# Attention and HGRN2 values: four weight lots at once, 512 moving columns instead of 256, in a decoder trunk on one core

## Chip, core and metric

One core of one Trainium2 chip runs the whole program as one launch. The metric is device time in microseconds (us), lower is better.

## What is computed

Two layers of a hybrid decoder trunk, 512 tokens of width 1024, all in float32. Each layer is a half-step SwiGLU (1024 to 2816 and back), a mixing stage with four branches of width 512, and a second half-step SwiGLU:

```python
h = rms_norm(x, mix_norm[l])
p = h @ w_in[l]
p_m2, p_s5, p_dsa, p_hg = jnp.split(p, IN_SPLITS, axis=-1)
y_a, y_b = mamba2_branch(p_m2, ...), s5_branch(p_s5, ...)
y_c, y_d = dsa_branch(p_dsa, ...), hgrn2_branch(p_hg, ...)
proj = jnp.einsum("blgc,gcd->blgd", ys, w_branch[l])
gates = jax.nn.sigmoid(h @ w_gate[l]).reshape(b, L, N_BRANCHES, D_MODEL)
x = x + jnp.einsum("blgd,blgd->bld", gates, proj) @ w_out[l]
```

The change touches two of the projections in `h @ w_in`: the attention values `v` (512 columns) of `dsa_branch`, and the HGRN2 values `i` (512 columns, called `hv` here) of `hgrn2_branch`. Both are needed with the tokens on the partitions, so for them the activations are the stationary operand and the weights move.

## The kernel before

Every weight matrix is streamed as *lots* of 128 x 1024 values (512 KB) through a ring of four slots: SP issues the DMA into `raw`, ACT rounds the lot to `w_hi` (`split_hi`, L461), POOL or DVE forms `w_lo = raw - w_hi` (`split_lo`, L469), and TensorE (PE) then makes three passes, hi·hi, lo·hi and hi·lo. A normal lot of a projection is 8 K tiles x 3 passes = 24 matmuls of 512 token columns (`passes`, L615 to L617). Output number t goes to PSUM bank t % 4. PE waits until that bank is free (semaphores `free0` to `free3`) and counts `out_done` when a sum is complete; ACT or DVE empties the bank. Banks 4 to 7 serve the branches' own small matmuls. The weights of lot n+4 may be split only when PE has used lot n.

The order of the work of a mixing stage is a hand-written list of steps, `script()`. Each engine walks it in order and does its share of each step, so a step's place sets its place on all queues. The steps that matter here:

- `("pair", "v", i)`, `("pair", "hv", i)`: the token-by-token product (`gemm_tokens`, L643 to L645) for two lots, i and i+1. For each of four blocks of 128 tokens, the stationary operand is `h_hi[:, k, tok]` or `h_lo`, the moving one 2 x 128 weight columns. That is 96 matmuls of 256 columns, two per projection and so eight in all. Two blocks share a bank; both lots are released only at the pair's end. ACT copies the two banks out (L1806) and then splits two lots.
- `glu` i: two sums of 12 matmuls each (a linear one, then its gate) for the S5 branch. ACT takes the gate's bank with a tanh (`glu_th`, L1928). DVE frees the linear bank in `glu_mul` (`glu_y`, L2729). ACT and DVE make `y_hi` (L1797) and `y_lo` (L2554) in `glu_end`.
- `da_index` b: 8 small matmuls (L1012), ACT's `da_r` (L1963), and on DVE the scores `da_mb` (L2765 to L2772). `da_rope`, `da_norm`, `da_topk` are further steps of the attention branch, the first and last on DVE alone.
- `gate` and `branch`: projections by `w_gate` and `w_branch`; `branch` 1, 0 is the first user of the S5 result and waits for `y_done` before each of its first four K tiles.
- `lot` hf, hq, hg: HGRN2's forget, query and output-gate projections; `hg_gates` and `hg_head` are its recurrence, head by head.

Of the kernel before, what the change touches and what calls it, by code (L numbers as in the profile page):

```python
# [51 lines left out]
def script():  # L52
# [36 lines left out]
    s += [("s5_end",), ("lot", "qi", 1), ("da_rope", 0, 2, 4), ("lot", "k", 3), ("da_index", 1), ("da_square", 1), ("glu", 0)]  # L89
# [77 lines left out]
for _i, (_kind, _j) in enumerate(MIX):  # L167
    if _kind in ("v", "hv") and _j % 2 == 0:

        USED_AT[MIX0 + _i] += 1  # L170
        assert all((MIX0 + _i + _l * NLOT) % 4 != 3 for _l in range(DEPTH)), (_kind, _j, (MIX0 + _i) % 4)
# [45 lines left out]
def trunk(nc, x_in, positions, w_lots, par_in, s5_in, con_in, gamma_in, out, s5_taps, s5_ud, s5_wd):  # L217
# [5 lines left out]
    with ctx:  # L223
# [228 lines left out]

        def split_hi(act, n0, it=0, taken=False):
# [4 lines left out]
            if n0 >= 4 and not taken:  # L458
                act.wait_ge(S["out_done"], USED_AT[n0 - 4] + 4 * it + OUT.layer * OUT0[NLOT])
# [11 lines left out]
        LOADED = 16  # L471
# [119 lines left out]
        def _(pe):  # L591
# [38 lines left out]
            def gemm_tokens(n0, cols, lots=1):  # L630

                s, w = slot(n0), P * lots
                pe.wait_ge(S["lo_done"], LOT(n0 + lots))
                per = NB // lots
                for b in range(NB):
                    t = OUT[n0] + b // per
                    if b % per == 0:
                        pe.wait_ge(S["free%d" % (t % 4)], t // 4)
                    o = bank[t % 4][:, w * (b % per):w * (b % per) + (cols if lots == 1 else w)]
                    tok = slice(P * b, P * (b + 1))  # L640
                    wh, wl = (w_[:, s:s + lots, :, 0:cols] for w_ in (w_hi, w_lo))
                    for k in range(KT):
                        pe.matmul(o, h_hi[:, k, tok], wh[:, :, k], start=(k == 0), stop=False)  # L643
                        pe.matmul(o, h_lo[:, k, tok], wh[:, :, k], start=False, stop=False)  # L644
                        m = pe.matmul(o, h_hi[:, k, tok], wl[:, :, k], start=False, stop=(k == KT - 1))  # L645
                    if b % per == per - 1:
                        m.then_inc(S["out_done"], 1)
# [244 lines left out]
            def pair(kind, i):  # L892
                gemm_tokens(LOT_AT[(kind, i)], P, 2)
# [348 lines left out]
            STEPS = dict(lot=lot, pair=pair, turn_small=turn_small, out=out, out_start=out_start, glu=glu, glu_mul=glu_mul, glu_end=glu_end,  # L1242
# [197 lines left out]
        def _(pool):  # L1440
# [90 lines left out]
        def _(act):  # L1531
# [267 lines left out]
            def pair(kind, i):  # L1799

                n, dst = LOT_AT[(kind, i)], da_v if kind == "v" else hv
                for half in range(2):
                    t = OUT[n] + half
                    wait_out(act, t)
                    src = bank[t % 4][:, :].rearrange("p (b m) -> p b m", b=2)
                    act.activation(dst[:, 2 * half:2 * half + 2, P * i:P * (i + 2)], src, AFT.Copy) \  # L1806
                       .then_inc(S["free%d" % (t % 4)], 1)
                split_hi(act, n + 4)
                split_hi(act, n + 5)
# [1407 lines left out]
```

## Time and profile before

| | |
|---|---|
| median of 3 runs | 2758.59 us (2758.49 to 2758.92) |
| profiled execution: time | 2758.63 us |
| profiled execution: span of its instructions | 2756.8 us |
| PE busy (matmuls) | 2751.4 us, 16438 matmuls |
| PE busy loading weights | 2356.6 us |
| DVE / ACT / POOL busy | 1836.7 / 1331.1 / 927.3 us |

Times in the trace count from the span's start. A matmul's recorded duration runs from its start to its modelled end, and the matmuls overlap, so what one costs PE in a stream is the distance from one start to the next. The mixing stage of the first layer lies at about 380 to 930 us, that of the second at about 1750 to 2300 us.

### The profile page before, as it was taken

The page shows a single profiled execution, that of the slowest core. Times are in us where ns is not written, and L with a number is a line of the kernel's source. Part 1 is how long each engine was busy: PE and PEld are TensorE (multiplying, and loading weights), DVE is VectorE, ACT ScalarE, POOL GpSimd, SP SyncE. Part 2 cuts the span into 40 slices and gives each one's busy share as a digit, 9 for nine tenths or more (in the row PEclk, how much of TensorE's full clock was granted, in tenths as well). Part 3 has the DMA queues.
Part 4 walks back from the last instruction along what each step waited for, and adds up shares of the span by engine and source line. Part 5 has one row for each costly group of instructions (what it writes and reads, how often), then busy time and mean ns, then how long its engine had stood idle before and what let it go on. Part 6 is the DMA issues. An engine that isn't in the chain of part 4 may idle for free.

```text
span 2756.8 us, 42589 instructions
## 1 busy us (share of the span) xinstructions
PE 2751.4 (100%) x16438; PEld 2356.6 (85%) x16438; DVE 1836.7 (67%) x2982; ACT 1331.1 (48%) x2095; POOL 927.3 (34%) x458
## 2 busy tenths in 40 slices
PE   9999999999999999999999999999999999999999
PEld 8898888877788888898998988888777888898988
DVE  7686857685667448585785868576856674585755
ACT  6353444555355446353563535445553553453533
POOL 0135823333333442131121367234333334421321
PEclk9999999999999999999999999999999999999999
DMA  5333583222222232232332335832222222322332
GB/s 170 107 108 115 155 181 100 79 75 70 84 85 85 84 99 94 92 115 100 108 107 92 115 117 161 166 100 88 74 76 78 77 92 85 100 94 98 108 98 102
DMA packets 113111, 284.84 MB, mean 103 GB/s; under 512 B 35616, under 2 KB 45344, under 8 KB 112416
## 3 DMA queue, kind: packets, MB, share of 16 engines
q1 hardware_dynamic: 112928, 282.35, 33.5%
q8 instruction: 122, 2.00, 0.3%
q14 instruction: 61, 0.50, 0.1%
HBM read 268.67 MB, written 9.44 MB: 101 GB/s over the span
## 4 chain that ended last, share of the span: by engine, by line
PE 98%; DVE 1%; ACT 0%; issue 0%; DMA 0%; SPq 0%; DVEq 0%; ACTq 0%
PE bank L615 22%; PE bank L616 22%; PE bank L617 22%; PE bank L664 7%; PE bank L665 7%; PE bank L666 7%; PE bank L643 1%; PE bank L644 1%; PE bank L645 1%; PE bank L1025 1%; PE bank L1044 1%; PE bank L1059 1%; PE bank L805 1%; PE bank L1158 1%; PE bank L999 0%; PE bank L1012 0%
## 5 line engine op out<-in xcount | busy, mean ns | idle before, releaser
L469 POOL TENSOR_TENSOR w_lo<-raw,w_hi 128x1024 fp32r<-128x1024 f32 x208 | 519.4, 2502 | 895.5 <-ACT w_hi L461 895.5
L615 PE MATMUL bank<-h_hi,w_hi 128*128 128x512 f32 x1504 | 593.2, 394 | 0.4 <-DVE silu_a L2324 0.3
L617 PE MATMUL bank<-h_hi,w_lo 128*128 128x512 f32 x1504 | 585.9, 390 | 0.0
L616 PE MATMUL bank<-h_lo,w_hi 128*128 128x512 f32 x1504 | 585.7, 389 | 0.0
L535 POOL TENSOR_TENSOR w_lo<-raw,w_hi 128x1024 fp32r<-128x1024 f32 x122 | 223.5, 1855 | 802.0 <-DVE bank L2269 802.0
L461 ACT ACTIVATE w_hi<-raw 128x1024 fp32r<-128x1024 f32 x310 | 325.7, 1055 | 341.8 <-PE bank L617 320.0
L615 PEld LDWEIGHTS bank<-h_hi,w_hi 128*128 128x128 f32 x1504 | 282.3, 188 | 64.9 <-issue 6.7
L617 PEld LDWEIGHTS bank<-h_hi,w_lo 128*128 128x128 f32 x1504 | 282.3, 188 | 59.7
L616 PEld LDWEIGHTS bank<-h_lo,w_hi 128*128 128x128 f32 x1504 | 282.5, 188 | 56.5
L615 PE MATMUL bank<-g_hi,w_hi 128*128 128x512 f32 x698 | 271.9, 390 | 0.0
L616 PE MATMUL bank<-g_lo,w_hi 128*128 128x512 f32 x698 | 271.7, 389 | 0.0
L617 PE MATMUL bank<-g_hi,w_lo 128*128 128x512 f32 x698 | 271.5, 389 | 0.0
L1578 ACT ACTIVATE t_hi<-bank 128x512 fp32r<-128x512 f32 x244 | 145.0, 599 | 196.9 <-DVE bank L2267 61.2
L469 DVE TENSOR_TENSOR w_lo<-raw,w_hi 128x1024 fp32r<-128x1024 f32 x102 | 148.2, 1453 | 97.6 <-ACT w_hi L461 97.4
L664 PE MATMUL bank<-s_hi,t_hi 128*128 128x256 f32 x732 | 207.1, 283 | 0.1
L666 PE MATMUL bank<-s_hi,t_lo 128*128 128x256 f32 x732 | 206.4, 282 | 0.0
L665 PE MATMUL bank<-s_lo,t_hi 128*128 128x256 f32 x732 | 206.3, 282 | 0.0
L530 ACT ACTIVATE w_hi<-raw 128x1024 fp32r<-128x1024 f32 (+1 forms) x168 | 149.5, 897 | 85.8 <-PE bank L666 59.7
L2283 DVE TENSOR_TENSOR t_lo<-bank,t_hi 128x512 fp32r<-128x512 f32 x244 | 167.6, 687 | 28.0 <-ACT t_hi L1578 19.1
L617 PEld LDWEIGHTS bank<-g_hi,w_lo 128*128 128x128 f32 x698 | 131.0, 188 | 27.4
L615 PEld LDWEIGHTS bank<-g_hi,w_hi 128*128 128x128 f32 x698 | 131.1, 188 | 27.3 <-issue 0.4
L616 PEld LDWEIGHTS bank<-g_lo,w_hi 128*128 128x128 f32 x698 | 131.1, 188 | 26.6
(447 smaller groups left out, 6008.8 us busy)
## 6 DMA issues: line engine op xcount, KB each, us to landing
raw<-in_w_lots SPq DMA_DIRECT2D x478, 512.0 KB, 3.6
s_wd<-s_z SPq DMA_DIRECT2D x8, 512.0 KB, 2.7
s_t<-s_taps SPq DMA_DIRECT2D x16, 256.0 KB, 12.9
da_s<-da_qk SPq DMA_DIRECT2D x16, 256.0 KB, 3.9
x<-in_x SPq DMA_DIRECT2D x8, 256.0 KB, 5.7
raw_k<-in_w_lots SPq DMA_DIRECT2D x8, 256.0 KB, 6.1
s_w_im<-s_wd SPq DMA_DIRECT2D x32, 64.0 KB, 3.9
s_w_re<-s_wd SPq DMA_DIRECT2D x32, 64.0 KB, 2.8
```

The costliest lines, as they stand in the source:

```text
L461: act.activation(w_hi[:, s], raw[:, s], AFT.Copy).then_inc(S["hi_done"], 1)
L469: eng.tensor_tensor(w_lo[:, s], raw[:, s], w_hi[:, s].bitcast(f32), SUB).then_inc(S["lo_done"], 1)
L530: act.activation(w_hi[:, s, k0:KT], raw[:, s, k0:KT], AFT.Copy).then_inc(S["hi_done"], 1)
L535: eng.tensor_tensor(w_lo[:, s, k0:KT], raw[:, s, k0:KT], w_hi[:, s, k0:KT].bitcast(f32), SUB).then_inc(S["lo_done"], 1)
L615: pe.matmul(b[:, :], w_hi[:, s, kw], xh[:, k], start=(k == 0), stop=False)
L616: pe.matmul(b[:, :], w_hi[:, s, kw], xl[:, k], start=False, stop=False)
L617: return pe.matmul(b[:, :], w_lo[:, s, kw], xh[:, k], start=False, stop=(k == nk - 1))
L664: pe.matmul(o, hi[:, k0 + k], x_hi[:, x0 + k, cols], start=start and k == 0, stop=False, skip_group_check=True)
L665: pe.matmul(o, hi[:, k0 + k], x_lo[:, x0 + k, cols], start=False, stop=False, skip_group_check=True)
L666: m = pe.matmul(o, lo[:, k0 + k], x_hi[:, x0 + k, cols], start=False, stop=(k == 3), skip_group_check=True)
L1578: act.activation(t_hi[parity(n)][j][:, :, :], sums_bank(j), AFT.Copy).then_inc(S["x0_in_t_hi"], 1)
L2283: TT(t_lo[q][j][:, :, :], sums_bank(j), t_hi[q][j][:, :, :].bitcast(f32), SUB).then_inc(S["w0_in_t_lo"], 1)
```

## The change

Both values are now made by one step, `("tokens", kind)`, over all four lots. On the host the four lots are rearranged so that each holds two K tiles for all 512 output columns (as the first four lots of the program already did). PE goes through the lots, e = 0 to 3. In each, it adds the lot's two K tiles to four running sums, one for each block of tokens, in all four banks. One matmul has 512 moving columns. After each of the first three lots a new count, `x2_in_piece`, releases that lot; the sums are complete during the fourth. ACT splits three further lots as they are released, then copies four banks out, then splits the fourth.

The script moves: `glu_mul` 0 stands right behind `glu` 0; all of v stands behind `da_index` 2 and ahead of `da_rope` 1, `da_index` 3 and `glu` 1; the two places behind `glu_mul` 1 and `da_topk` 1, 3 where a v pair stood are empty. All of hv stands ahead of `hg_head` 0, 0, with hf 2 and hf 3 moved from ahead of the hq lots to where the second hv pair stood.

```diff
-    s += [..., ("lot", "k", 3), ("da_index", 1), ("da_square", 1), ("glu", 0)]
-    s += [("da_index", 2), ("glu_mul", 0), ("da_rope", 1, 0, 4), ("glu", 1), ("da_index", 3)]
+    s += [..., ("lot", "k", 3), ("da_index", 1), ("da_square", 1), ("glu", 0), ("glu_mul", 0)]
+    s += [("da_index", 2), ("tokens", "v"), ("da_rope", 1, 0, 4), ("da_index", 3), ("glu", 1)]
     s += [("glu_end", 0), ("glu_mul", 1)]
-    s += [("pair", "v", 0), ("glu_end", 1)] + topk(1, 0, 2) + [("da_norm", 0), ("glu", 2), ("glu_mul", 2), ("da_norm", 1)]
-    s += [("glu", 3), ("glu_end", 2), ("glu_mul", 3)] + topk(1, 2, 4) + [("pair", "v", 2), ("m2_decay",), ("glu_end", 3)]
+    s += topk(1, 0, 2) + [("da_norm", 0), ("glu_end", 1), ("glu", 2), ("glu_mul", 2), ("da_norm", 1)]
+    s += [("glu", 3), ("glu_end", 2), ("glu_mul", 3)] + topk(1, 2, 4) + [("m2_decay",), ("glu_end", 3)]
...
-    fill = [("lot", "hg", 0), ("pair", "hv", 2)] + [("lot", "hg", i) for i in (1, 2, 3)] + merges(0)
-    s += [("pair", "hv", 0)]
+    fill = [("lot", "hg", 0), ("lot", "hf", 2), ("lot", "hf", 3)] + [("lot", "hg", i) for i in (1, 2, 3)] + merges(0)
...
+            if isinstance(it, int) and n0 - 4 in BY_TOKENS and BY_TOKENS[n0 - 4] % 4 < 3:
+                act.wait_ge(S["x2_in_piece"], piece_at(n0 - 4))
...
+            def gemm_tokens(n0):
+                for e in range(4):
+                    sl = slot(n0 + e)
+                    pe.wait_ge(S["lo_done"], LOT(n0 + e + 1))
+                    for b in range(NB):
+                        t, tok = OUT[n0] + b, slice(P * b, P * (b + 1))
+                        if e == 0:
+                            pe.wait_ge(S["free%d" % (t % 4)], t // 4)
+                        for k in (2 * e, 2 * e + 1):
+                            wh, wl = (w_[:, sl, 4 * (k % 2):4 * (k % 2) + 4].rearrange("p j m -> p (j m)") for w_ in (w_hi, w_lo))
+                            pe.matmul(bank[t % 4][:, :], h_hi[:, k, tok], wh, start=(k == 0), stop=False)
+                            pe.matmul(bank[t % 4][:, :], h_lo[:, k, tok], wh, start=False, stop=False)
+                            m = pe.matmul(bank[t % 4][:, :], h_hi[:, k, tok], wl, start=False, stop=(k == KT - 1))
+                        if e == 3:
+                            m.then_inc(S["out_done"], 1)
+                    if e < 3:
+                        m.then_inc(S["x2_in_piece"], 1)
...
+            def tokens(kind):
+                n, dst = LOT_AT[(kind, 0)], da_v if kind == "v" else hv
+                for e in range(3):
+                    split_hi(act, n + 4 + e)
+                for b in range(NB):
+                    t = OUT[n] + b
+                    wait_out(act, t)
+                    act.activation(dst[:, b], bank[t % 4][:, :], AFT.Copy).then_inc(S["free%d" % (t % 4)], 1)
+                split_hi(act, n + 7)
```

Where it moves instructions, first DVE around `glu_mul` 0 in the first layer (`da_mb` are the attention scores of blocks 1 and 2, `da_s` is the rope; in brackets the semaphores waited for). Before:

```order
L2769 SCALAR_TENSOR_TENSOR da_mb<-da_r,small,da_mb 128x256 [waits da_relu,dve_seq]
L2772 TENSOR_TENSOR da_mb<-da_mb,con 128x128 [waits da_score]
L2765 TENSOR_SCALAR da_mb<-da_r,small 128x384 [waits da_relu,dve_seq]
L2767 SCALAR_TENSOR_TENSOR da_mb<-da_r,small,da_mb 128x384 [waits da_relu,dve_seq] x2
L2769 SCALAR_TENSOR_TENSOR da_mb<-da_r,small,da_mb 128x384 [waits da_relu,dve_seq]
L2772 TENSOR_TENSOR da_mb<-da_mb,con 128x128 [waits da_score]
L2729 SCALAR_TENSOR_TENSOR glu_y_153<-glu_th,bank 128x512 [waits free0,out_done,dve_seq]
```

And with the change:

```order
L2771 SCALAR_TENSOR_TENSOR da_mb<-da_r,small,da_mb 128x256 [waits da_relu,dve_seq]
L2774 TENSOR_TENSOR da_mb<-da_mb,con 128x128 [waits da_score]
L2731 SCALAR_TENSOR_TENSOR glu_y_153<-glu_th,bank 128x512 [waits free0,out_done,dve_seq]
L2767 TENSOR_SCALAR da_mb<-da_r,small 128x384 [waits free3,da_relu]
L2769 SCALAR_TENSOR_TENSOR da_mb<-da_r,small,da_mb 128x384 [waits da_relu,dve_seq] x2
L2771 SCALAR_TENSOR_TENSOR da_mb<-da_r,small,da_mb 128x384 [waits da_relu,dve_seq]
```

`glu_mul` 0 moves ahead of the scores of block 2, but stays behind those of block 1. Then ACT from `glu` 0 on. Before:

```order
L1928 ACTIVATE glu_th<-bank 128x512 [waits out_done]
L461 ACTIVATE w_hi<-raw 128x1024 [waits raw_in3,out_done]
L1963 ACTIVATE da_r<-bank 128x384 [waits da_score,da_rel]
L1963 ACTIVATE da_r<-bank 128x384 x3
L1928 ACTIVATE glu_th<-bank 128x512 [waits out_done]
L461 ACTIVATE w_hi<-raw 128x1024 [waits raw_in0,out_done]
L1963 ACTIVATE da_r<-bank 128x512 [waits da_score,da_rel]
```

With the change:

```order
L1930 ACTIVATE glu_th<-bank 128x512 [waits out_done]
L465 ACTIVATE w_hi<-raw 128x1024 [waits raw_in3,out_done]
L1965 ACTIVATE da_r<-bank 128x384 [waits da_score,da_rel]
L1965 ACTIVATE da_r<-bank 128x384 x3
L465 ACTIVATE w_hi<-raw 128x1024 [waits raw_in0,x2_in_piece]
L465 ACTIVATE w_hi<-raw 128x1024 [waits raw_in1,x2_in_piece]
L465 ACTIVATE w_hi<-raw 128x1024 [waits raw_in2,x2_in_piece]
L1810 ACTIVATE da_v<-bank 128x512 [waits out_done] x4
L465 ACTIVATE w_hi<-raw 128x1024 [waits raw_in3,out_done]
L1965 ACTIVATE da_r<-bank 128x512 [waits da_score,da_rel]
```

Three splits that wait for PE's pieces, and four copies of the values, now stand between the `da_r` of blocks 2 and 3. The PE queue in the first lot of v, third block of tokens and start of the fourth (w_hi and w_lo move, h is stationary), with the change:

```order
L644 MATMUL bank<-w_hi,h_hi 128x512 [waits free3]
L645 MATMUL bank<-w_hi,h_lo 128x512
L646 MATMUL bank<-w_lo,h_hi 128x512
L644 MATMUL bank<-w_hi,h_hi 128x512
L645 MATMUL bank<-w_hi,h_lo 128x512
L646 MATMUL bank<-w_lo,h_hi 128x512
L644 MATMUL bank<-w_hi,h_hi 128x512 [waits free0]
```

The first two blocks stand ahead of these with `free1` and `free2`, six matmuls each; `free3` is the bank that `glu_mul` 0 gives back.

## Rows read from the trace of the kernel before

**Rows 1.** The page: PE busy and granted clock in 40 slices, the chain by engine

```profile
PE   9999999999999999999999999999999999999999
...
PEclk9999999999999999999999999999999999999999
...
PE 98%; DVE 1%; ACT 0%; issue 0%; DMA 0%; SPq 0%; DVEq 0%; ACTq 0%
```

**Rows 2.** Groups by line and form, PE: count, busy us, mean ns, idle before

```profile
L643 PE MATMUL bank<-w_hi,h_hi 128*128 128x256 f32 x256 | 72.8, 284 | 0.2
```

**Rows 3.** Timeline of PE: first matmul of each pair, first behind (start, us)

```profile
473.51 0.35 PE L643 MATMUL bank<-w_hi,h_hi 128*128 128x256 f32 x1
...
485.10 1.02 PE L999 MATMUL bank<-da_tq,con 128*128 128x512 f32 x2
...
502.91 0.28 PE L643 MATMUL bank<-w_hi,h_hi 128*128 128x256 f32 x1
...
514.42 0.40 PE L615 MATMUL bank<-h_hi,w_hi 128*128 128x512 f32 x1
...
798.08 0.28 PE L643 MATMUL bank<-w_hi,h_hi 128*128 128x256 f32 x1
...
809.59 0.61 PE L1197 MATMUL bank<-hq,he 128*128 128x128 f32 x4
...
817.59 0.39 PE L643 MATMUL bank<-w_hi,h_hi 128*128 128x256 f32 x1
...
829.20 0.50 PE L1225 MATMUL bank<-hv,hatt 128*128 128x128 f32 x3
```

**Rows 4.** Timeline of PE: second and last matmul of one normal lot

```profile
642.92 0.40 PE L616 MATMUL bank<-h_lo,w_hi 128*128 128x512 f32 x1
...
647.91 0.39 PE L617 MATMUL bank<-h_hi,w_lo 128*128 128x512 f32 x1
```

**Rows 5.** Timeline of PE: `da_index` 2, `glu` 1 behind it in both layers

```profile
464.33 1.56 PE L1012 MATMUL bank<-da_ki,da_qi 64*128 64x384 f32 x8
465.82 0.50 PE L615 MATMUL bank<-gel_hi,w_hi 128*128 128x512 f32 x1
...
1837.78 0.50 PE L615 MATMUL bank<-gel_hi,w_hi 128*128 128x512 f32 x1
```

**Rows 6.** Timeline of DVE: scores of block 1, `glu_mul` 0 in both layers

```profile
465.71 3.02 DVE L2767 SCALAR_TENSOR_TENSOR da_mb<-da_r,small,da_mb 128x256 f32<-128x256 f32 x2
...
469.28 0.29 DVE L2772 TENSOR_TENSOR da_mb<-da_mb,con 128x128 f32<-128x128 f32 x1
...
472.68 0.69 DVE L2729 SCALAR_TENSOR_TENSOR glu_y<-glu_th,bank 128x512 f32<-128x512 f32 x1
...
1841.34 0.29 DVE L2772 TENSOR_TENSOR da_mb<-da_mb,con 128x128 f32<-128x128 f32 x1
```

**Rows 7.** Timeline of POOL beside rows 6

```profile
466.05 2.39 POOL L469 TENSOR_TENSOR w_lo<-raw,w_hi 128x1024 fp32r<-128x1024 f32 x1 [2.85 <-ACT w_hi L461]
```

**Rows 8.** Timeline of DVE and ACT: from the end of `glu` 3 to `y_lo` 3

```profile
506.72 2.47 DVE L2554 SCALAR_TENSOR_TENSOR y_lo<-glu_y,y_hi 128x512 fp32r<-128x512 f32 x1 [1.02 <-ACT y_hi L1797]
...
514.10 0.19 DVE L2832 SCALAR_TENSOR_TENSOR m_dt<-m_dt 128x32 f32<-128x32 f32 x1
...
517.01 0.20 ACT L2028 ACTIVATE m_ea<-par 128x8 f32<-128x8 f32 x1
...
518.77 0.62 ACT L1797 ACTIVATE y_hi<-glu_y 128x512 fp32r<-128x512 f32 x1
```

**Rows 9.** Timeline of PE: `att_start`, and `branch` 1, 0 behind it

```profile
525.42 0.72 PE L1025 MATMUL bank<-da_qk 64*128 64x128 f32 x8
526.06 0.50 PE L615 MATMUL bank<-y_hi,w_hi 128*128 128x512 f32 x1
```

**Rows 10.** Timeline of DVE and PE: the recurrence of `hg_head` 0 and its user

```profile
828.85 1.11 DVE L2994 SCALAR_TENSOR_TENSOR hS<-hS,hdec,bank 128x128 f32<-128x128 f32 x3 [0.15 <-DVE hS L2994]
...
830.19 1.07 PE L1229 MATMUL bank<-hS,hq 128*32 128x128 f32 x30
```

More of the change, by code:

```diff
@@ L121, in script @@
         ahead = [[("hg_gates", h + 1, phase)] if h < 3 else [] for phase in range(3)]
-        s += [("hg_head", h, 0)] + ahead[0] + take(fill, 1) + [("hg_head", h, 1)] + take(fill, 1) + ahead[1]
+        s += [("hg_head", h, 0)] + ahead[0] + take(fill, 1) + [("hg_head", h, 1)] + take(fill, 1 if h else 2) + ahead[1]
         s += (take(fill, 1) if h else []) + [("hg_head", h, 2), ("hg_scale", h)] + ahead[2]
@@ L137, in mix_lots @@
             lots.append(step[1:])
-        elif step[0] == "pair":
-            lots += [(step[1], step[2]), (step[1], step[2] + 1)]
+        elif step[0] == "tokens":
+            lots += [(step[1], i) for i in range(4)]
         elif step[0] == "quad":
@@ L166 @@
 USED_AT = [OUT0[_n + 1] for _n in range(NLOT)]
[L167 to L171, printed above, removed]
+BY_TOKENS = {MIX0 + _i: 4 * ("v", "hv").index(_kind) + _j for _i, (_kind, _j) in enumerate(MIX) if _kind in ("v", "hv")}
 FIRST_LOT = [[at0 + 2 * sum(THIRDS[:_th]) + KT * _th for _th in range(len(THIRDS))] for at0 in (0, FFN2_0)]
@@ L628, in gemm_first @@
                             m.then_inc(S["out_done"], 1)
[L630 to L647, printed above, removed]
+            def gemm_tokens(n0):
[15 more added lines that the diff above has]
+                        m.then_inc(S["x2_in_piece"], 1)
             def norm_sums(r):
@@ L1240, in hg_end @@
                 pass
-            STEPS = dict(lot=lot, pair=pair, turn_small=turn_small, out=out, out_start=out_start, glu=glu, glu_mul=glu_mul, glu_end=glu_end,
+            STEPS = dict(lot=lot, tokens=tokens, turn_small=turn_small, out=out, out_start=out_start, glu=glu, glu_mul=glu_mul, glu_end=glu_end,
                          gate=gate, branch=branch, merge=merge, da_square=da_square,
@@ L1508, in mixing @@
                         after(*step[1:])
-                    elif step[0] == "pair":
-                        after(step[1], step[2])
-                        after(step[1], step[2] + 1)
+                    elif step[0] == "tokens":
+                        for i in range(4):
+                            after(step[1], i)
                     elif step[0] == "quad":
@@ L1797, in split_y, with tokens @@
                 act.activation(y_hi[:, i], src, AFT.Copy, scale=scale).then_inc(S["y_hi_done"], 1)
[L1799 to L1803, printed above, removed]
-                    wait_out(act, t)
[L1805 to L1809, printed above, removed]
+            def tokens(kind):
+                n, dst = LOT_AT[(kind, 0)], da_v if kind == "v" else hv
[3 more added lines that the diff above has]
+                    t = OUT[n] + b
+                    wait_out(act, t)
+                    act.activation(dst[:, b], bank[t % 4][:, :], AFT.Copy).then_inc(S["free%d" % (t % 4)], 1)
+                split_hi(act, n + 7)
             def lot(kind, i):
@@ L2139, in hg_end @@
                 split_y(3, h, hf[:, h], scale=0.5)
-            STEPS = dict(lot=lot, pair=pair, turn_small=turn_small, out=out, out_start=out_start, glu=glu, glu_mul=glu_mul, glu_end=glu_end,
+            STEPS = dict(lot=lot, tokens=tokens, turn_small=turn_small, out=out, out_start=out_start, glu=glu, glu_mul=glu_mul, glu_end=glu_end,
                          gate=gate, branch=branch, merge=merge, da_square=da_square,
@@ L2558, in lot, with tokens @@
                 pass
-            def pair(kind, i):
+            def tokens(kind):
                 pass
@@ L3018, in _ @@
             layer_at = [None]
-            STEPS = dict(lot=lot, pair=pair, turn_small=turn_small, out=out, out_start=out_start, glu=glu, glu_mul=glu_mul, glu_end=glu_end,
+            STEPS = dict(lot=lot, tokens=tokens, turn_small=turn_small, out=out, out_start=out_start, glu=glu, glu_mul=glu_mul, glu_end=glu_end,
                          gate=gate, branch=branch, merge=merge, da_square=da_square,
```

22 lines of the change are left out of this document (12 added, 10 removed).

## Prediction

> **What bounds the kernel now.** I read the page first: PE is busy in all 40 slices, the granted clock is full throughout (the upper of the two levels, 2.4 GHz), and the chain of waits lies on PE for 98% of the span [rows 1]. So the time is the sum of the distances between matmul starts. Only two things can change it: fewer or cheaper matmuls, and PE waiting. The view by line gives the size of what is replaced: three lines of 256 matmuls with 256 columns, 768 in all, with next to no idle time before them [rows 2]. Their mean of 284 ns is not their cost, since they overlap. The timeline of PE gives that. A pair of 96 matmuls takes 514.42 - 502.91 = 11.51 us, and 809.59 - 798.08 = 11.51 us; the two pairs that follow small float32 matmuls take 11.59 and 11.61 us, 0.1 us more for the entry [rows 3]. So one costs 11.51 / 96 = 119.9 ns. In a normal lot 22 distances with 512 columns last 647.91 - 642.92 = 4.99 us, or 226.8 ns each [rows 4].
>
> **Step 1, the matmuls.** The columns in total stay the same, the count halves: 768 become 384. Per layer the four pairs take 11.59 + 11.51 + 11.51 + 11.61 = 46.22 us. The new ones take 192 x 0.2268 = 43.55 us, and I leave two entries of 0.1 us: v still stands behind small matmuls, and hf 2 now stands where the second hv pair did. That is 43.75 us, so 2.5 us less per layer and **4.9 us less** in two. Read another way, two matmuls of 256 columns cost 2 x 119.9 = 239.8 ns and one of 512 costs 226.8 ns: each matmul has a part of about 13 ns that does not grow with the columns. The trace has no matmul of 512 columns with h stationary; the bounds are 226.8 ns (the same columns, the other operand stationary) and 239.8 ns (two of the old ones), that is 4.9 us to nothing. I take the lower, since the count of rows and columns is the same as in the lot.
>
> Here a rule speaks against the change. The Trainium skill, in "TensorE: Matmul & The Clock Gate", section "Back-to-back issue gap", gives N / 2.4 + 2.5 ns at the full clock: an estimate from it is 109.2 ns for 256 columns and 215.8 ns for 512, and by it the edit would save 768 x 109.2 - 384 x 215.8 ns = 1.0 us, not 4.9. The trace disagrees, with 119.9 and 226.8 ns.
>
> **Step 2, the four banks of v.** This is where I expect a new wait. A pair needed two banks, the first at its start. The new step needs all four within its first lot: block b of tokens starts 6 x b matmuls in. The bank of the third block is the one that held `glu` 0's linear sum, two outputs earlier, and DVE gives it back in `glu_mul` 0. PE's queue now has v directly behind `da_index` 2, so v takes the place of `glu` 1 and starts at 465.82 us [rows 5]. The third block is due 12 x 0.2268 + 0.1 = 2.8 us later, at 468.6. DVE is then still on the scores of block 1, stretched because POOL's `w_lo` runs beside them: two operations take 3.02 us [rows 6, 7], and nothing in the change is ahead of this point, so both stay. The scores end at 469.28 + 0.29 = 469.57. Only then does `glu_mul` 0 run, 0.69 us, to about 470.3. Before, it ended at 472.68 + 0.69 = 473.37 and the pair that needed it started at 473.51 [rows 3, 6], so add 0.14: PE goes on at 470.4. **PE waits 1.8 us.** In the second layer v starts at 1837.78 [rows 5], its third block is due at 1840.6, the scores end at 1841.34 + 0.29 = 1841.63 [rows 6], and the bank comes at 1842.5: 1.9 us. Together **+3.7 us**. Without moving `glu_mul` 0 ahead of the scores of block 2 it would be over 3 us more per layer (472.68 instead of about 469.6), which is why that edit is part of the price and brings no gain of its own. Bounds: 0, if DVE gets there 1.8 us earlier, and 4.9 us per layer, if it came where it comes now. The order of DVE's queue speaks for the value in between.
>
> The fourth block's bank (`glu` 0's gate, emptied by ACT behind PE's gate sum) is long free. The copies of v and the three splits that wait for pieces stand on ACT ahead of `da_r` 3, so ACT is bound to PE's pace for some 22 us. Behind it are `da_r` 3, needed by PE only at `da_norm` 0, one glu lot later, and `y_hi` 0, needed much later: nothing. Each lot is released one by one, every 24 x 0.2268 = 5.4 us, instead of two at once after 11.5 us, so weights come earlier than before: nothing.
>
> **Step 3, the cover of the S5 result.** Before, a v pair of 11.5 us stood on PE between `glu` 3 and the first gate lot, and hid what ACT and DVE do to `y_lo` 3. It is gone; what is late next is `branch` 1, 0, at its fourth K tile. From the end of `glu` 3 on PE the cover is now two gate lots, 48 x 0.2268 = 10.9, plus `att_start`, 526.06 - 525.42 = 0.64 [rows 9], plus nine matmuls, 2.0, and an entry: 13.7 us. The chain: before, `glu` 3 ended at 502.91 [rows 3], and DVE went through `y_lo` 2, `glu_mul` 3, the top-k phases and `m2_decay` to 514.10 + 0.19 = 514.29 [rows 8], 11.4 us later; nothing among them waited for the pair. Then ACT's `m2_decay`, 518.77 - 517.01 = 1.8, `y_hi` 3, 0.6 [rows 8], and `y_lo` 3, 0.7 as the same shape in rows 6: 14.5 us. That is 0.8 us late. But ACT enters the norms with less ahead of it than before (two splits and two copies of a v pair stood there), so the chain may be as much as 0.8 us shorter. Bounds 0 to 0.9 us per layer with the semaphore's delay; I take 0.3, **+0.6 us** in two.
>
> **Step 4, hv.** Four banks at once are no trouble here: the four outputs ahead of it are the hq lots, which ACT copies out as they come. The tightest place behind is `hg_head` 0, 2: DVE's recurrence ends at 828.85 + 1.11 = 829.96 and PE uses it from 830.19 [rows 10], a margin of 0.2 us. PE gets there 1.3 us earlier. DVE's start hangs on ACT's work behind the hv copies, which moves by as much, so I cost it at 0; if DVE did not move at all PE would wait 1.1 us per layer.
>
> **Sum.** -4.9 + 3.7 + 0.6 = -0.6 us against the profiled execution's 2758.63 us, which lies 0.04 us above the median of the runs: **2758.0 us**. A measurement of this kernel can tell about 0.2%, 5.5 us, from no change, so this is no change.
>
> **Rivals.**
> - *The bank is free in time* (0.14). If `glu_mul` 0 meets the third block, step 2 is nothing: 2758.6 - 4.9 + 0.6 = 2754.3, or 2753.7 without step 3 too. Against it stand the scores that are ahead on DVE in both layers. Even this case stays just inside 0.2%; beyond it (under 2753.1) the rows show nothing more to remove.
> - *No saving in step 1* (0.08). If the new matmul costs 239.8 ns, what two old ones do, the time is 2758.6 + 3.7 + 0.6 = 2762.9. The skill's formula lies near this case with its 1.0 us, by which the time would be 2761.9.
> - *The S5 chain ends late, and it is slower* (0.08). DVE operations stretch when POOL's `w_lo` meets them: `y_lo` 2 took 2.47 us where the shape takes 0.69 [rows 6, 8], and block 1's scores as much. Two more such meetings in step 3's chain add 3.6 us, `branch` 1, 0 waits 4.5 us per layer, and the time is 2758.6 - 4.9 + 3.7 + 9.0 = 2766.4. It decides from a wait of 3.4 us per layer on, a chain of 17.1 us. For it speaks that the splits now come at other times; against it, that the chain of rows 8 already holds one meeting.
> - *The change does not do what it says* would show as a matmul count other than 16438 - 384 = 16054; what is built shows the single form of 512 columns, so I give it nothing.
>
> **How the numbers follow.** The forecast has 0.70. The range takes in the first rival and most of the hv and step 3 bounds: 2753.6 to 2762.0 us. Faster by over 0.2%: 0.06, a corner of the first rival. Slower by over 0.2%: 0.08, the third, with the rest of the second inside. Within 0.2%: 0.86.
>
> **What would show it.** PE: 384 matmuls of 128x512 with h stationary, distances of 227 ns, 43.5 us of them per layer. An idle stretch of PE of about 1.8 us, 12 matmuls into v in both layers, ended by DVE's `glu_y`; none 12 matmuls into hv. `branch` 1, 0 with a wait under 1 us before its fourth K tile, ended by DVE's `y_lo`. PE busy lower by about 5 us. I am wrong if the first stretch is missing, or if a wait of over 2 us stands anywhere else.

## The result, and the profile after

The changed kernel takes **2762.89 us** (median of 20 runs, 2762.33 to 2764.36) beside 2758.75 us of the kernel before (20 runs on the same chip, 2757.30 to 2759.66): a ratio of 1.0015, 95% interval 1.0009 to 1.0021. It is slower by 4.1 us, or 0.15%, and the interval excludes "no change" (a ratio of 1). The forecast was 2758.0 us, with a range from 2753.6 to 2762.0.

The spans of the two profiled executions differ by as much: 2760.8 against 2756.8 us. The page of the changed kernel, its busy times and its chain of waits by engine, beside the table of before and [rows 1]:

```profile
PE 2748.5 (100%) x16054; PEld 2336.1 (85%) x16054; DVE 1853.9 (67%) x2982; ACT 1331.8 (48%) x2095; POOL 927.2 (34%) x458
...
PEclk9999999999999999999999999999999999999999
...
PE 90%; DVE 6%; ACT 2%; issue 1%; DMA 0%; SPq 0%; DVEq 0%; ACTq 0%
```

There are 384 matmuls less, as the change says, and PE is busy 2.9 us less. The clock is full all the way (1.00 in this execution). What is new is the last line: before, the chain lay on PE for 98%, now for 90%, and DVE has 6% of it. PE now waits for something that it did not wait for before. The view of waits says for what (waiting instruction, whom it waited for, us in total, times, longest):

```profile
PE bank L644 <- DVE glu_y L2731: 3.0, 2, 1.5
PE bank L1047 <- ACT da_p L1984: 2.7, 4, 0.9
PE bank L1047 <- ACT da_pt L1993: 1.3, 6, 0.3
...
PE bank L1062 <- ACT da_o L2016: 0.6, 2, 0.3
```

The first line is the wait for the third bank of v, forecast in step 2. The other three stand in the attention units (the sixteen steps `att` of the script), where the kernel before has none; the groups left out here stand in the kernel before too. There are six of these waits in each layer, of 0.2 to 0.9 us each. The view counts only the idle time, 4.6 us in both layers. Against the timeline of before, by the starts of the matmuls, what they cost is 2.9 us per layer: PE is 0.31 us behind the kernel before when `glu` 3 has ended (the next lot starts at 514.73 against 514.42, [rows 3]), and 3.22 us behind at 715 us.

So the sum is: -4.9 us of matmuls, +3.4 us for the bank (1.69 and 1.68), +5.8 us in the attention units, together +4.3; measured +4.1. The bank's share is a little larger if the slower start of the matmuls behind the wait is put down to it: the step is 1.86 us shorter without the wait (e1), which makes +3.7 in two layers and a sum of +4.6.

**The v step.** Timeline of PE of the changed kernel (start us, duration us, engine, line, operation, out<-in, count, and in brackets the idle time before and who ended it), to hold beside [rows 3, 5]:

```profile
465.60 0.50 PE L644 MATMUL bank<-w_hi,h_hi 128*128 128x512 f32 x1
...
468.23 0.39 PE L646 MATMUL bank<-w_lo,h_hi 128*128 128x512 f32 x1
470.14 0.50 PE L644 MATMUL bank<-w_hi,h_hi 128*128 128x512 f32 x1 [1.52 <-DVE glu_y L2731]
...
489.44 1.99 PE L1015 MATMUL bank<-da_ki,da_qi 64*128 64x512 f32 x8
...
790.42 0.39 PE L644 MATMUL bank<-w_hi,h_hi 128*128 128x512 f32 x1
...
812.18 1.05 PE L1200 MATMUL bank<-hq,he 128*128 128x128 f32 x8
```

Twelve matmuls run, the thirteenth stands until `glu_mul` 0 has given the bank back: 470.14 - 468.23 = 1.91 us where 0.23 is usual, so the wait costs 1.68 to 1.69. The step takes 489.44 - 465.60 = 23.84 us, and 22.15 with those 1.69 taken off; hv takes 812.18 - 790.42 = 21.76 and waits nowhere.

**The attention units.** Here are the two engines that feed them. First in the kernel before, ACT, one split of POOL, and then DVE, from `m2_decay` to the first merge of group 1 (`m_ea` is ACT's first operation of `m2_decay`, `gate_th` a gate lot's tanh, `da_p` an exponential of unit 0, `m_dt` and `m_dp` belong to the step `m2_dt`, `merged` is the merge):

```profile
517.01 0.20 ACT L2028 ACTIVATE m_ea<-par 128x8 f32<-128x8 f32 x1
...
520.70 0.60 ACT L1870 ACTIVATE gate_th<-bank 128x512 f32<-128x512 f32 x1
...
526.97 0.39 ACT L1974 ACTIVATE da_p<-da_p,da_st 128x128 f32<-128x128 f32 x1
...
527.15 2.40 POOL L469 TENSOR_TENSOR w_lo<-raw,w_hi 128x1024 fp32r<-128x1024 f32 x1 [2.42 <-ACT w_hi L461]
...
528.34 1.25 DVE L2837 SCALAR_TENSOR_TENSOR m_dt<-m_dt 128x32 f32<-128x32 f32 x1
529.63 0.29 DVE L2839 SCALAR_TENSOR_TENSOR m_dp<-m_dt,m_ea 128x32 f32<-128x32 f32 x2
...
533.84 0.69 DVE L2593 SCALAR_TENSOR_TENSOR merged<-gate_th,bank 128x512 f32<-128x512 f32 x1
```

And the same steps in the changed kernel, with POOL's splits beside them at the end:

```profile
525.22 0.21 ACT L2030 ACTIVATE m_ea<-par 128x8 f32<-128x8 f32 x1 [7.64 <-DVE m_dt L2834]
...
528.92 0.60 ACT L1872 ACTIVATE gate_th<-bank 128x512 f32<-128x512 f32 x1
...
531.79 0.40 ACT L1976 ACTIVATE da_p<-da_p,da_st 128x128 f32<-128x128 f32 x1
...
532.32 0.16 DVE L2801 RECIPROCAL da_st<-da_st 128x1 f32<-128x1 f32 x1 [2.40 <-ACT da_p L1976]
...
533.16 2.19 DVE L2839 SCALAR_TENSOR_TENSOR m_dt<-m_dt 128x32 f32<-128x32 f32 x1
535.39 2.40 DVE L2841 SCALAR_TENSOR_TENSOR m_dp<-m_dt,m_ea 128x32 f32<-128x32 f32 x2
...
541.72 0.69 DVE L2595 SCALAR_TENSOR_TENSOR merged<-gate_th,bank 128x512 f32<-128x512 f32 x1
...
530.55 7.10 POOL L473 TENSOR_TENSOR w_lo<-raw,w_hi 128x1024 fp32r<-128x1024 f32 x3 [11.02 <-ACT w_hi L465]
```

Before the change, ACT comes to `m2_decay` at 517.01 from the copies and splits of the v pair, without a wait: DVE's part had been done since 514.29 [rows 8]. Now there is no pair, ACT is there early and stands **7.64 us** until DVE is through its top-k phases. Everything behind it on ACT, the gates and the first exponentials, is late, DVE waits 2.40 us for those, and its small operations of `m2_dt` then fall into three splits of POOL in a row, which come in a row because POOL had waited 11.02 us for ACT's late `w_hi`. The merge comes 541.72 - 533.84 = 7.9 us late. Of this, 531.79 - 526.97 = 4.8 us is the lateness of the exponentials; the rest is `m_dt` (2.19 us, where it had met one split before and took 1.25) and `m_dp` (2.40 us for two, before 0.29). PE itself is only 0.3 us late at the first lot behind `glu` 3; from the merge on DVE and ACT lag behind PE and hand several units over late, the last at 598.6 us. The first lot behind `glu` 3, the place where PE first feels the lateness, and the largest single wait:

```profile
514.73 0.39 PE L618 MATMUL bank<-h_hi,w_hi 128*128 128x512 f32 x1
...
544.44 0.33 PE L1047 MATMUL bank<-con,da_p 128*128 128x128 f32 x1 [0.51 <-ACT da_p L1984]
...
588.81 0.44 PE L1047 MATMUL bank<-con,da_p 128*128 128x128 f32 x2 [0.88 <-ACT da_p L1984]
```

### The profile page after: what moved, and what is told of

It is laid out like the page before. It is cut to its first block, busy times and chain, and to the rows that moved or that the text cites. A ratio compares the mean times of both kernels' runs of the same rounds, so it can differ in the third digit from the quotient of the medians.

```text
span 2760.8 us, 41815 instructions
## 1 busy us (share of the span) xinstructions
PE 2748.5 (100%) x16054; PEld 2336.1 (85%) x16054; DVE 1853.9 (67%) x2982; ACT 1331.8 (48%) x2095; POOL 927.2 (34%) x458
## 4 chain that ended last, share of the span: by engine, by line
PE 90%; DVE 6%; ACT 2%; issue 1%; DMA 0%; SPq 0%; DVEq 0%; ACTq 0%
PE bank L618 20%; PE bank L620 20%; PE bank L619 20%; PE bank L667 7%; PE bank L668 7%; PE bank L669 7%; DVE da_mb L2780 1%; DVE da_m L2779 1%; PE bank L644 1%; PE bank L646 1%; PE bank L645 1%; PE bank L808 1%; PE bank L1161 1%; PE bank L1062 1%; PE bank L1047 1%
```

## The experiments

Each kernel was timed beside the kernel before (11 runs each, but 5 of e8 and 6 of e9), whose median was 2758.93, 2758.78 and 2758.67 us in the three groups of four. The changed kernel's 2762.89 is the other mark.

**First group: which part costs what.**

*e1: the bank wait taken away alone.* Only DVE's own queue is changed.

```diff
# DVE alone
-for step in SCRIPT:
+steps = list(SCRIPT)
+steps.remove(("glu_mul", 0))
+steps.insert(steps.index(("da_index", 1)), ("glu_mul", 0))
+for step in steps:
```

> The changed kernel, with glu_mul 0 ahead of the scores of block 1 in DVE's queue alone. Theory A (two separate waits: the bank of v's third block, 1.7 us per layer, and a DVE that is late in the attention, 2.9 us per layer, for its own reasons): the bank wait goes, the attention's stay, so 3.4 us less than the changed kernel, 2759.5 us. Rival B (the attention's waits only follow from the bank wait's delay): both go, 2762.9 - 3.4 - 5.8 = 2753.7 us. Rival C (the bank was not what PE waited for): 2762.9 us, with the stretch of 1.7 us still there.

Measured: 2759.97 us, ratio 1.0004 (0.9995 to 1.0013). The wait of `glu_y` is gone and PE is 1.86 us earlier behind v. The loss in the attention units stays, 3.3 us per layer instead of 2.9. So there are two causes, and this one can be taken away without the other; e6 below does the reverse.

*e2 and e3: one half of the change each.* e2 has the v pairs of before and only hv token by token with its reordering, e3 the reverse.

```diff
# e2: rows of v as before the change
-    s += [("da_index", 2), ("tokens", "v"), ("da_rope", 1, 0, 4), ("da_index", 3), ("glu", 1)]
+    s += [("da_index", 2), ("glu_mul", 0), ("da_rope", 1, 0, 4), ("glu", 1), ("da_index", 3)]
...
# e3: rows of hv as before the change
-    s += [("hg_gates", 0, 1), ("m2_end",), ("hg_start",), ("hg_gates", 0, 2), ("tokens", "hv")]
+    s += [("pair", "hv", 0)]
```

> The part on hv alone: hv by tokens and its reordering, v in pairs at its old places. If the parts add, it takes 1.3 us per layer off the kernel before and adds no wait: 2758.7 - 2.6 = 2756.1 us. Rival (the halved count brings nothing and the change of the sum came from elsewhere): 2758.7 us.

> The part on v alone: v by tokens at its new place, hv in pairs at the old ones. If the parts add: 2762.9 + 2.6 = 2765.5 us, that is 3.4 us per layer over the kernel before (1.2 saved in the matmuls, 1.7 for the bank, 2.9 in the attention). Rival (part of the attention's waits come with hv's share): under 2763 us.

Measured: e2 2756.02 us, ratio 0.9989 (0.9980 to 0.9998); e3 2765.32 us, ratio 1.0023 (1.0014 to 1.0032). hv alone gains 2.9 us and brings no wait, v alone loses 6.4, and -2.9 + 6.4 = +3.5 is about what the two do together (+4.1). All of the loss is in v.

*e4: the idle time ahead filled.* DVE was idle 6.5 us behind the rope, ahead of `da_index` 3, so two top-k phases were put there.

```diff
-    ..., ("da_rope", 1, 0, 4), ("da_index", 3), ("glu", 1)]
+    ..., ("da_rope", 1, 0, 4)] + topk(1, 0, 2) + [("da_index", 3), ("glu", 1)]
...
-    s += topk(1, 0, 2) + [("da_norm", 0), ...
+    s += [("da_norm", 0), ...
```

> The changed kernel, with the first two top-k phases of block 1, 3.9 us of DVE work that needs nothing from the others, moved ahead of da_index 3, into the 6.5 us in which DVE has nothing to do behind the rope. Theory A1 (the attention's waits come from a DVE that is late, for having stood idle there): DVE is up to 3.9 us earlier at the attention's start and most of the 2.9 us per layer go: 2762.9 - 5 = 2758 us; the bank wait of 1.7 us per layer stays. Rival A2 (ACT, bound to PE's pieces during v, is what is late): no change, 2762.9 us.

Measured: 2763.51 us, ratio 1.0016 (1.0007 to 1.0025): nothing gained, theory A1 falls. (Rival A2 of this run forecast that time, but its cause, ACT bound to PE's pieces during v, is not it either: e6 leaves v as it is and has no wait in the units. From e5 on, A2 names another theory.) The trace shows why nothing was gained: DVE is idle again further on, where the phases stood. Its waits from 475 to 530 us:

```profile
DVE y_lo L2556 <- ACT y_hi L1800: 6.2, 3, 2.8
DVE da_qk L2755 <- ACT da_tk L1958: 5.5, 1, 5.5
DVE da_mb L2767 <- ACT da_r L1965: 2.8, 1, 2.8
DVE da_qk L2755 <- ACT da_tq L1958: 2.6, 1, 2.6
```

In the changed kernel the wait at the second norm (`da_tk`) is 1.8 us, here 5.5: what DVE gained ahead of the norm it stood idle at it. What makes the units late must hang behind it, on the end of `glu` 3.

**Second group: what hangs on the end of `glu` 3.**

*e5: all four top-k phases early*, so that the two (3.9 us) between `glu_mul` 3 and `m2_decay` are gone from there.

```diff
-    ..., ("da_rope", 1, 0, 4), ("da_index", 3), ("glu", 1)]
+    ..., ("da_rope", 1, 0, 4)] + topk(1, 0, 4) + [("da_index", 3), ("glu", 1)]
...
-    ..., ("glu_mul", 3)] + topk(1, 2, 4) + [("m2_decay",), ("glu_end", 3)]
+    ..., ("glu_mul", 3), ("m2_decay",), ("glu_end", 3)]
```

> The changed kernel, with all four top-k phases of block 1 that stood ahead of the S5 result (two behind glu_end 0, two behind glu_mul 3) put ahead of da_index 3 on DVE, where DVE was idle 6.5 us. Theory A2: the waits in the attention units come from what hangs on the end of glu 3 on DVE and ACT (y_lo 2, glu_mul 3, two top-k phases, m2_decay, y_hi and y_lo 3, gates, first exponentials), for which a v pair of 11.5 us was cover before. Then 3.9 us of top-k less in that row brings m2_decay, the gates and the merges 3.9 us earlier, DVE's y_lo 3 at about 523.8 instead of 527.6, half of the 7.9 us that merge 1,0 is late; the 2.9 us of PE waits per layer shrink to under 1, and the time is 2758 to 2760. Theory B (it is the meetings of DVE with POOL's w_lo in the attention units, or the total of DVE's work there, which was moved by nothing of this): waits stay over 2 us per layer, 2762 to 2763. The bank wait of 1.7 us per layer at the third block of v stays in either.

Measured: 2757.19 us, ratio 0.9995 (0.9985 to 1.0004), 5.7 us less than the changed kernel. There is no wait of PE left in the attention units.

*e6: only the order turned round.* The same work, `m2_decay` ahead of the two phases.

```diff
-    ..., ("glu_mul", 3)] + topk(1, 2, 4) + [("m2_decay",), ("glu_end", 3)]
+    ..., ("glu_mul", 3), ("m2_decay",)] + topk(1, 2, 4) + [("glu_end", 3)]
```

> The changed kernel, with m2_decay ahead of the two top-k phases behind glu_mul 3 (DVE and ACT alike). DVE's total ahead of the attention units is the same, but ACT no longer stands 7.6 us before m2_decay, so its exponentials for the first units no longer wait for DVE's top-k. Theory A2a (ACT's queue is what makes attention late): gates and first exponentials about 3 us earlier, PE waits in the units fall from 2.9 to about 1 us per layer, 2759 to 2760. Theory A2b (it is DVE's row, whatever ACT does): merge 1,0 on DVE stays at about 541.7 us, waits stay, 2762.5 to 2763.

Measured: 2757.11 us, ratio 0.9995 (0.9985 to 1.0004), 5.8 us less. This is the sharpest of the runs, since DVE does as much ahead of the units as in the changed kernel and the gain is all the same. Theory A2a is right in kind, but it had forecast a gain of only 3 to 4 us. The timeline of ACT, DVE and POOL in e6:

```profile
521.64 0.21 ACT L2030 ACTIVATE m_ea<-par 128x8 f32<-128x8 f32 x1 [3.71 <-DVE m_dt L2834]
...
525.35 0.60 ACT L1872 ACTIVATE gate_th<-bank 128x512 f32<-128x512 f32 x1
...
528.22 0.40 ACT L1976 ACTIVATE da_p<-da_p,da_st 128x128 f32<-128x128 f32 x1
...
529.59 2.18 DVE L2839 SCALAR_TENSOR_TENSOR m_dt<-m_dt 128x32 f32<-128x32 f32 x1
531.81 0.29 DVE L2841 SCALAR_TENSOR_TENSOR m_dp<-m_dt,m_ea 128x32 f32<-128x32 f32 x2
...
536.01 0.69 DVE L2595 SCALAR_TENSOR_TENSOR merged<-gate_th,bank 128x512 f32<-128x512 f32 x1
...
526.97 4.75 POOL L473 TENSOR_TENSOR w_lo<-raw,w_hi 128x1024 fp32r<-128x1024 f32 x2 [7.07 <-ACT w_hi L465]
```

The merge is 541.72 - 536.01 = 5.7 us earlier than in the changed kernel. 528.92 - 525.35 = 3.6 of it is ACT's shorter stand; the other 2.1 is the second meeting with POOL that no longer happens (`m_dp` 2.40 us, now 0.29). How much of the 5.8 us of time each of the two would give alone was not tried.

*e7: e5 and e1 together.*

> The four top-k phases early, as in the run before, and glu_mul 0 ahead of the scores of block 1 on DVE, which alone took 2.9 us off. If the two causes are apart, the gains add: 2.9 us under the top-k version; by theory A2 about 2756, by theory B 2760.

Measured: 2753.61 us, ratio 0.9982 (0.9973 to 0.9991). The two causes add up, and this is faster than both kernels.

*e8: v between the second norm and `glu` 3*, with `da_index` 3 and `glu` 1 as before the change.

```diff
...
+    s += [("da_index", 2), ("glu_mul", 0), ("da_rope", 1, 0, 4), ("glu", 1), ("da_index", 3)]
...
     s += [("glu_end", 0), ("glu_mul", 1)]
+    s += topk(1, 0, 2) + [("da_norm", 0), ("glu_end", 1), ("glu", 2), ("glu_mul", 2), ("da_norm", 1), ("glu_end", 2)]
+    s += [("tokens", "v")] + topk(1, 2, 4) + [("m2_decay",), ("glu", 3), ("glu_mul", 3), ("glu_end", 3)]
```

> The changed kernel, with the step v standing behind da_norm 1 and glu_end 2 instead of behind da_index 2; behind it the two top-k phases, m2_decay and then glu 3, as the matmuls of 512 columns alone. da_index 3 and glu 1 stand as before the change. The third block of v then needs the bank of glu 2, whose product DVE made before the norm, so no bank wait of note; top-k and m2_decay have the 21.8 us of v as cover, and behind glu 3 only glu_mul 3 and y_hi, y_lo 3 hang, about 3 us under 13 us of two gate lots. Theory A2: neither the 1.7 nor the 2.9 us per layer: before less 4.9, 2754 to 2755. Theory B: the bank wait is gone but the waits in the units are not: 2759 to 2760. A wait elsewhere (ACT's copies of v, bound to PE's pace, hold up the norm's second half or da_o's first unit) would show as a new stretch of PE in front of that step.

Measured: 2772.50 us, ratio 1.0052 (1.0038 to 1.0066). The expectation missed by 18 us. It had counted the work that v would cover, and not what v's old place had covered: nothing stands on PE now between `da_index` 3 and the first norm, whose banks ACT has not yet emptied, and behind the second norm the bank of `glu` 2 is not free. PE waits 2.17 and 3.66 us there. Each wait costs more than itself, as the view by stretches shows for e8 (stretch, sum, busy times by engine with counts, granted clock, DMA share and rate):

```profile
475.00:476.00 1.00, 0.58 (x1) 0.50 (x2) 1.00 (x2) 0.98 (x3) 0.33 (x1) 0.68 0.00 0
476.00:478.00 2.00, 2.00 (x3) 0.67 (x2) 1.97 (x4) 1.65 (x2) 0.00 (x0) 0.50 0.66 176
478.00:480.00 2.00, 2.00 (x5) 0.91 (x4) 1.97 (x4) 0.95 (x3) 0.00 (x0) 0.81 0.24 94
480.00:482.00 2.00, 2.00 (x9) 1.32 (x8) 1.97 (x4) 1.81 (x3) 0.00 (x0) 1.00 0.00 0
...
496.00:498.00 2.00, 1.93 (x5) 1.55 (x6) 1.77 (x4) 1.73 (x4) 0.00 (x0) 0.50 0.00 0
```

Behind both waits the granted clock is 0.50, the lower of the two levels (1.2 GHz). The eight matmuls of the norm take 480.20 - 475.42 = 4.78 us against 488.25 - 485.10 = 3.15 in the kernel before, and those of v stand 0.43 us apart at first, instead of 0.23. The second layer has the same two waits (2.2 and 3.6 us). Per layer that is 2.17 + 3.66 + 1.6 + 1.6 = 9.0 us, 18.1 in two, and 2753.4 (e12, below) + 18.1 = 2771.5, which leaves 1.0 us unexplained.

**Third group: the price, the cover, the best version.**

*e9: the matmuls halved again*, order and waits as in the change.

```diff
-    pe.matmul(bank[t % 4][:, :], h_hi[:, k, tok], wh, ...)
...
+    for c in (slice(0, 256), slice(256, 512)):
+        o = bank[t % 4][:, c]
+        pe.matmul(o, h_hi[:, k, tok], wh[:, c], ...)
...
```

> The changed kernel with each matmul of 512 columns in the steps v and hv made as two of 256 columns, six matmuls per K tile and block instead of three; order, banks and waits untouched. Theory of step 1: the price is in the matmul count alone, 239.8 ns for two of 256 columns against 226.8 for one of 512, so 384 x 13 ns = 5.0 us more, 2767.9 by the changed kernel's 2762.9; the new pairs of matmuls then stand 119.9 ns apart. Rival (part of the saving comes from something else in the new form, such as the four weight lots being released one by one): less than 4 us more.

Measured: 2768.03 us, ratio 1.0034 (1.0022 to 1.0046), 5.1 us over the changed kernel: 13.4 ns for each of the 384. Its timeline has the halves 0.12 us apart:

```profile
466.48 0.28 PE L646 MATMUL bank<-w_hi,h_hi 128*128 128x256 f32 x1
466.60 0.28 PE L647 MATMUL bank<-w_hi,h_lo 128*128 128x256 f32 x1
466.72 0.28 PE L648 MATMUL bank<-w_lo,h_hi 128*128 128x256 f32 x1
```

*e10: the kernel before, its second v pair moved ahead of `glu` 3.* No matmul changes its form here.

```diff
-    ..., ("glu_mul", 2), ("da_norm", 1)]
-    s += [("glu", 3), ("glu_end", 2), ("glu_mul", 3)] + topk(1, 2, 4) + [("pair", "v", 2), ("m2_decay",), ("glu_end", 3)]
+    ..., ("glu_mul", 2), ("da_norm", 1), ("pair", "v", 2)]
+    s += [("glu", 3), ("glu_end", 2), ("glu_mul", 3)] + topk(1, 2, 4) + [("m2_decay",), ("glu_end", 3)]
```

> The kernel before, with its second v pair moved from behind glu 3 to ahead of it (behind da_norm 1), nothing else. The cover behind glu 3 is gone as in the change, but here the pair lies between the norm and glu 3, so the norm's exponentials on ACT and its multiplications on DVE are done when glu 3 ends. Theory A2 (what counts is the whole row on DVE and ACT from norm 1 on to the gates): after glu 3's end at 514.4 come y_lo 2, glu_mul 3, two top-k phases, m2_decay, about 7 us, to 521, which is 4 us earlier than in the changed kernel and about as in the two versions without waits: no wait in the attention units, 2758.5 to 2759.5. Rival A3 (any loss of the pair behind glu 3 costs the 2.9 us per layer): 2764 to 2765.

Measured: 2763.50 us, ratio 1.0018 (1.0009 to 1.0027). Rival A3 (2764 to 2765) is right but for 0.5 us, A2 in the form stated there is wrong. The trace has the changed kernel's picture on the old matmuls:

```profile
515.80 0.62 ACT L1797 ACTIVATE y_hi<-glu_y 128x512 fp32r<-128x512 f32 x1
524.06 0.21 ACT L2028 ACTIVATE m_ea<-par 128x8 f32<-128x8 f32 x1 [7.64 <-DVE m_dt L2832]
...
516.45 2.47 DVE L2554 SCALAR_TENSOR_TENSOR y_lo<-glu_y,y_hi 128x512 fp32r<-128x512 f32 x1 [11.00 <-ACT y_hi L1797]
...
540.58 0.69 DVE L2593 SCALAR_TENSOR_TENSOR merged<-gate_th,bank 128x512 f32<-128x512 f32 x1
```

DVE sat idle 11.0 us during the pair, because `y_hi` 2 stands on ACT behind `glu` 3's tanh; the row begins only when `glu` 3 ends, and what was done ahead of it does not matter. From that end (514.16) to `m2_decay` on DVE it takes 9.9 us, not the 7 that I had counted: I had left out the tanh ahead of `y_hi` 2 and the stretched `y_lo` 2.

*e11: two lots of xbc as cover* behind `glu` 3, taken out of the attention units' fill.

```diff
-    ..., ("glu_mul", 3)] + topk(1, 2, 4) + [("m2_decay",), ("glu_end", 3)]
+    ..., ("glu_mul", 3)] + topk(1, 2, 4) + lots(("xbc", 2)) + [("m2_decay",), ("glu_end", 3)]
...
+    fill = [f for f in fill if f not in lots(("xbc", 2))]
```

> The changed kernel, with two lots of xbc (10.9 us on PE) taken out of the fill of the attention units and put where the second v pair stood, behind glu 3; DVE's and ACT's work keeps its order. Theory A2: with 10.9 us of cover back, the gates and the first units find DVE and ACT as before the change; 5.8 us of waits go, 2757, less what the attention units lose at their end where two lots of fill are now missing. Theory B (DVE's or ACT's total in the units decides): no gain, or worse by the waits at the end of the units, 2763 or more.

Measured: 2758.47 us, ratio 0.9999 (0.9990 to 1.0008), 4.4 us less. ACT comes to `m2_decay` without a wait again, and the waits on `da_p` are gone. In their place is a new one at the end of the units (669.3 us), where the lots are missing, so that PE still loses 0.7 us per layer. PE's two largest groups of waits in the whole of e11 (the first is v's bank; the three smaller ones stand in the kernel before too):

```profile
PE bank L645 <- DVE glu_y L2732: 3.0, 2, 1.5
PE bank L1063 <- ACT da_pt L1994: 1.4, 2, 0.7
```

*e12: the changed kernel with e6's order and e1's.*

> The changed kernel with the two cheap edits together: glu_mul 0 ahead of the scores of block 1 on DVE, and m2_decay ahead of the two top-k phases. 2.9 us and 5.8 us are apart, so 2762.9 - 8.7 = 2754.2, beside 2753.6 of the version with four early top-k phases. If it is under 2753, the two edits help each other; if over 2756, one of them takes from the other.

Measured: **2753.44 us** (11 runs, 2752.73 to 2754.62), ratio 0.9982 (0.9973 to 0.9991). Its chain of waits lies on PE for 99%, and the v step runs through:

```profile
PE 99%; DVE 1%; ACT 0%; DMA 0%; issue 0%; SPq 0%; DVEq 0%; ACTq 0%
```

```profile
466.20 0.50 PE L644 MATMUL bank<-w_hi,h_hi 128*128 128x512 f32 x1
...
488.18 1.99 PE L1015 MATMUL bank<-da_ki,da_qi 64*128 64x512 f32 x8
```

The lateness of the merge and PE's loss go together over all these versions. The third column is the merge's start on DVE less PE's own shift against the kernel before at 514.42 (for e11 its two lots are in that shift); the last is what PE falls further behind the kernel before until 715 us, per layer:

```
kernel    merge start   PE's shift   late by   PE loses, 514 to 715 us
before         533.84         0          0      0
e11            544.63       +10.8        0      0.7 (in other places)
e12            534.39        -0.9       1.5     0.0
e5             538.62        +3.3       1.5     0.0
e6             536.01        +0.7       1.5    -0.1
e10            540.58        -0.3       7.0     2.7
e1             540.65        -0.8       7.6     3.3
after          541.72        +0.3       7.6     2.9
```

The shift of e5 is so large because its profiled execution was one of 2759.74 us, with a wait of 2.2 us near the program's start; the median is 2757.19. Nothing was measured between 1.5 and 7 us late, so where in between the waits begin is open.

## Why the prediction was wrong, step by step

**Step 1, the matmuls, was right.** The steps measured 21.98 us (v in e12, without the wait) and 21.76 us (hv), together 43.74 us per layer against 43.75. e9 gives the price from the other side, 13.4 ns a matmul against "about 13 ns". The rival *no saving in step 1* named 2762.9 us, which is the time that came out, but that is a coincidence: by its reason e9 would have changed nothing.

**Step 2, the four banks of v, was right.** Forecast: 1.8 and 1.9 us, twelve matmuls in, ended by `glu_y`. Measured: 1.69 and 1.68, at that place and by that cause; 3.4 us for 3.7, or 3.7 by what e1 takes off the step. The rival of the free bank is out. The edit that would have avoided it lay close by: the forecast noted that the scores of block 1 stand ahead of `glu_mul` 0 on DVE, and exactly their exchange (e1) removes it.

**Step 3, the cover, is the one that failed.** Its working followed the right chain of work, from the end of `glu` 3 through `m2_decay` to `y_lo` 3, and its length was about right: `y_lo` 3 ends at 527.64 + 0.69 = 528.33, 13.6 us after `glu` 3, where 14.5 was reckoned. The deadline it was held against, `branch` 1, 0, was met too, with no wait at all. What was wrong is "what is late next is `branch` 1, 0": that is only one of the users, and it was not the one that was late. Behind `m2_decay` on ACT stand the gates and unit 0's exponentials, behind those on DVE the `m2_dt` operations, two top-k phases and the merge, and then all the units. The step gave the cover a price of 0.3 us per layer with a bound of 0.9; it was 2.9. The one sentence that looked at ACT counted only that it would come *earlier*; [rows 8] held what was needed, DVE done with `m2_decay` at 514.29 and ACT coming at 517.01 from a v pair's copies. Take those away, and ACT is there first and stands before DVE's top-k with all that is queued behind it.

**The third rival** had the sign and named lengthening by POOL's splits. Two such meetings stand there (`m_dt`, which had one of 1.25 us before already, and `m_dp`), and they add 3 us to the merge's lateness. But its mechanism, `branch` 1, 0 waiting 4.5 us, did not happen.

**Step 4, hv, was right.** No wait at any place, and e2 gives 2.9 us; half the matmuls were reckoned at 2.4 to 2.5.

**The sign of being wrong that the prediction named** would have missed it, read by the letter: "if a wait of over 2 us stands anywhere else". No single wait in the units is over 0.9 us. They are six per layer, and only their sum, 2.9 us per layer, is over 2. A sign should have been set on the sum of PE's new waits in a stretch, not on one wait.

**The size of what can be told apart** was put too large. The time did stay within 0.2%, as the prediction gave at 0.86, but it called that "no change", and 4.1 us is a change: the interval of the ratio, 1.0009 to 1.0021, does not reach 1.

With 2.9 in place of 0.3 the prediction's own sum is -4.9 + 3.7 + 5.8 = +4.6, 2763.2 us, 0.3 us from the result.

## What to carry to other kernels

When work is taken off the engine that bounds the kernel, list everything that it covered on the *other* engines' queues, not only the next operand: a step whose data are ready late holds up all that is queued behind it there, and where those engines are nearly full afterwards, the lateness is handed on unit after unit. A small step that one engine waits for (`m2_decay`, two operations of 0.2 us) belongs ahead of long work that nobody waits for yet (top-k). In the kernel before, with the cover, ACT did not wait for that step; here, without it, the order costs 5.8 us. And a loss of 0.15% can be two independent waits of known place and a gain that is real: with both taken away the change is worth 5.2 us against the kernel before.

## What the runs showed of the hardware

- A DVE operation on a tiny tile (128x32) took 2.19 us and two of them 2.40 us beside POOL's `w_lo` in the changed kernel, where two took 0.29 us without it (before, e6). Their ends, 535.35 and 537.79, lie at the ends of the second and third of POOL's three operations (530.55 + 2 x 2.37 = 535.29, and 537.65): in these rows the small operation does not share the time but ends when POOL's does. In e6, too, `m_dt` ends at 529.59 + 2.18 = 531.77 and POOL's pair at 531.72, and in the kernel before at 528.34 + 1.25 = 529.59 and POOL's split at 527.15 + 2.40 = 529.55. The Trainium skill, in "SBUF — State Buffer", section "SBUF: two separate sides", has this rule: a VectorE operation with two inputs in SBUF and a GpSimd operation that reads SBUF meet at a shared pair of ports, which is "an **exclusive lock**, not a bandwidth split", and the one that comes second blocks. `m_dt` and `m_dp` have two such inputs, and these rows agree.
- The wait of PE of 1.5 us (v's third bank) left the granted clock at 1.00. Behind the waits of 2.17 and 3.66 us in e8 it was 0.50 (476 to 478 us, mean 0.81 from 478 to 480; 496 to 498 us, mean 0.69 from 498 to 500), and the matmuls there took 1.6 us more each time, beside the wait itself. The six waits of each layer in the units, of 0.9 us and less, left it at 1.00 too. Where between 1.5 and 2.17 us this begins, and whether the length of the wait alone decides it, no run shows.
